# Seven products of halves in place of eight in the feed-forward up and gate products

## The chip, the core and the metric

One core of a Trainium2 chip. The metric is the device time of one execution in microseconds (us); several executions are measured and the median is given. TensorE (PE) multiplies, PEld is its weight load, VectorE is DVE, ScalarE is ACT, GpSimd is POOL, SyncE (SP) issues the transfers.

## The reference, cut to what matters

Two transformer blocks over 512 tokens of width 1024, all in float32. Each has mixers (attention of several kinds, a recurrence) and feed-forward parts, of which there are three:

```python
# first block, hidden width 4096
h2 = rmsnorm(x, norm_ffn_g[l])
x = x + jnp.square(jax.nn.relu(h2 @ w_ff1[l])) @ w_ff2[l]

# second block, twice, hidden width 2816
h = rms_norm(x, ffn_norm[i])
g, u = h @ w_gate[i], h @ w_up[i]
x = x + (jax.nn.silu(g) * u) @ w_down[i]
```

## The kernel before

Everything is kept as [features on 128 partitions, 512 tokens]. Each factor of a dense product is split in two float32r numbers, high = cast(value) on ScalarE and low = value - high on VectorE, and a product is three matmuls: high x high, low weight x high token, high weight x low token (L1075, L1078, L1081), all accumulated in one PSUM bank. Both PSUM and the matmuls work on 128 x 128 weights and 512 token columns.

The work is a list of `Unit`s. A `rows` unit is 128 output features (or 2 or 4 times 128) over `nk` blocks of 128 input features. `Plan.dense` cuts units into ticks: a tick is two weight blocks, that is six matmuls of 512 columns, followed by the steps of the other engines that go with it (`split`, `ev`, ...), some put off by some ticks with `defer`. All five engine programs walk through the same list `plan.steps` in the same order, and each engine does its own part of a step; they are held together by semaphores. So the order on each engine is fixed by hand, and an engine that waits holds up all that it has behind the wait.

Weights come in chunks of 512 KB over SP's queue into `raw0`/`raw1` (L2577); ScalarE casts a chunk to `wh` (L1503, `split`), VectorE makes `wl` (L1856, `split_low`), two buffers of each. The split of chunk n+2 is in the tick in which unit n ends.

A feed-forward stage is `chain(ff)`: groups of four 128-wide hidden tiles (two in the first group of the gated ones). In group c come the up units (in the gated stages gate and up alternate), then the output units of group c-1, which multiply the hidden tiles with the down weights and add to `x` (L2078). The tokens in `hh`, `hl` are not yet divided by their root mean square: the factor, in `W8`, is multiplied in when a bank is evicted (L2026 for relu, L1979 for gate and up). At the start of a stage that factor is not ready, so the first evictions are held back (`hold`). A gate's sigmoid is three dependent ScalarE instructions, Exp, Ln, Exp (L1602, L1612, L1616). Results are split again into the pair `R` (L1588, L1856). `F0` to `F8` are buffers of the mixers, unused within the feed-forward stages. The last output tile of the kernel is done in two halves of 256 tokens (`mm_half`, L1121 to L1123).

The part of the work that GpSimd has is small: additions in the gated mixing and in the recurrence (L2391, L2399, L2415).

Of the kernel before, what the change touches and what calls it, by code (L numbers as in the profile page):

```python
# [7 lines left out]
ALU = mybir.AluOpType  # L8
# [7 lines left out]
P = 128  # L16
T = 512
# [174 lines left out]

class Attn:
# [85 lines left out]
class Plan:  # L279
# [90 lines left out]
    def dense(self, units, more=None, crossed=False, hold=0):  # L370
# [5 lines left out]
        for u in units:  # L376
            if u.kind == "rows":
# [127 lines left out]

    def gate_up(self, n, y):
# [13 lines left out]
    def make(self):  # L520
# [14 lines left out]
        tile, self.f_tile = 0, []  # L535
        for c in range(8):
            self.f_tile.append(tile)
            up = [rows(("w_ff1", 0), 0, 8, c * 512 + j * P, P, ("h", 2), "relu2", f=c, j=j, tile=tile + j) for j in range(4)]
            ff1.append((up, self.out(("w_ff2", 0), 4 * c, 4, ("f", c), norm=2 if c == 7 else None)))
            tile += 4  # L540
        for idx, ff, e, norm in ((0, ff2a, 4, 4), (1, ff2b, 6, None)):
            for c in range(6):
                up, k0, nj, f = [], max(4 * c - 2, 0), 4 if c else 2, 8 + 6 * idx + c
                self.f_tile.append(tile)
                for j in range(nj):
# [3 lines left out]
                                      tile=tile + j)]  # L549
                ff.append((up, self.out(("w_down_2", idx), k0, nj, ("f", f), norm=norm if c == 5 else None,  # L550
# [36 lines left out]
        for units in stages:  # L587
            self.number(units)
# [38 lines left out]
        self.run(self.dense(chain(ff1), roots(1), hold=9))  # L627
# [13 lines left out]
        self.run(self.dense(chain(ff2a), roots(3), hold=9))  # L641
# [18 lines left out]
        self.run(self.dense(chain(ff2b), roots(5, tick=8), hold=10))  # L660
# [89 lines left out]
    dn_tb dn_q dn_s dn_r dn_o dn_p dt_t dt_a""".split()  # L750
# [14 lines left out]
class Memory:  # L765
    def __init__(self, nc, ctx):
# [11 lines left out]
        self.F = {f"F{i}": sb(f"F{i}", 2048) for i in range(9)}  # L778
# [89 lines left out]
    def pair(self, src):  # L868
# [5 lines left out]
        return self.R[2 * n], self.R[2 * n + 1]  # L874

# [165 lines left out]
def tensor_program(pe, S, B, plan):  # L1041
# [67 lines left out]
    def mm_half(u, a, b):  # L1109
# [14 lines left out]
        last.then_inc(S["mm"], 1)  # L1124

# [333 lines left out]
    def dt(u, h):  # L1459
# [10 lines left out]
            "sb": sb, "dt": dt}  # L1470
# [8 lines left out]
def scalar_program(act, S, B, plan, load_table, gains):  # L1479
# [352 lines left out]
    def dt(u, h):  # L1832
# [8 lines left out]
            "c_qt": c_qt, "c_kv": c_kv, "c_kt": c_kt, "sb": sb, "dn_sq": dn_sq, "dn_root": dn_root, "dt": dt}  # L1841
# [8 lines left out]
def vector_program(dve, S, B, plan):  # L1850
# [201 lines left out]
    def tile_low(u, w):  # L2052
# [4 lines left out]
        low(lo[:, js], w[:], hi[:, js], "f_lo")  # L2057

# [637 lines left out]
```

## Time and profile before

| | |
|---|---|
| median of 3 executions | 2140.13 us (2139.98 to 2140.21) |
| profiled execution, first to last instruction | 2138.5 us |
| TensorE busy | 2125.4 us, 99% |
| TensorE weight loads | 1685.6 us, 79% |
| VectorE busy | 1230.8 us, 58% |
| ScalarE busy | 914.8 us, 43% |
| GpSimd busy | 136.4 us, 6% |
| chain that ended last | TensorE 96%, VectorE 2%, ScalarE 1% |

The chain is followed back from the last instruction, at each step to what released it. Records of one engine overlap where it is pipelined: a busy time is that of the union of the records, and a mean is that of a single record.

### The profile page before, as it was taken

Reading aid. Unit: us, or ns where it says so; the run is one execution under the profiler, and the core shown is the slowest. Engines: PE = TensorE matmul, PEld = TensorE weight load, DVE = VectorE, ACT = ScalarE, POOL = GpSimd, SP = SyncE. Lnnn points to the kernel's source line nnn. Section 1 sums busy time; section 2 is a strip of 40 time slices with the busy share of each in tenths; the row PEclk is TensorE's granted clock in tenths of the full one; section 3 lists DMA queues with packets and bytes.
Section 4 is the critical chain, followed back from the end, with each engine's and each line's share of the span. In section 5 each row is a group of like instructions: output and inputs, shape, how many; then the busy total and the mean of one; then the engine's idle time right before and its main releaser. Section 6 shows DMA issues by size and latency. Waiting matters only on the chain.

```text
span 2138.5 us, 27352 instructions
## 1 busy us (share of the span) xinstructions
PE 2125.4 (99%) x10944; PEld 1685.6 (79%) x10944; DVE 1230.8 (58%) x1808; ACT 914.8 (43%) x1449; POOL 136.4 (6%) x174
## 2 busy tenths in 40 slices
PE   9999999999999999999999999999999999999999
PEld 7768778778888888887777888888877668888887
DVE  5584874565544444565676555555556676555554
ACT  4464544554433322334455433333445655333332
POOL 0000432211000000010111000000011100000000
DMA  5213212123222223222112322322221112222223
GB/s 171 84 56 89 61 45 102 40 85 114 98 99 90 98 99 98 99 89 79 60 60 70 99 93 95 99 99 99 89 89 60 59 40 99 99 99 99 89 99 108
DMA packets 52253, 186.91 MB, mean 87 GB/s; under 512 B 5920, under 2 KB 6432, under 8 KB 52000
## 3 DMA queue, kind: packets, MB, share of 16 engines
q1 hardware_dynamic: 51984, 184.99, 26.3%
q8 instruction: 87, 1.43, 0.3%
q14 instruction: 38, 0.31, 0.1%
q10 hardware_dynamic: 144, 0.18, 0.0%
HBM read 183.05 MB, written 2.10 MB: 87 GB/s over the span
## 4 chain that ended last, share of the span: by engine, by line
PE 96%; DVE 2%; ACT 1%; issue 1%; DMA 0%; SPq 0%; DVEq 0%; ACTq 0%
PE ps L1075 24%; PE ps L1078 24%; PE ps L1081 24%; PE ps L1099 4%; PE ps L1102 4%; PE ps L1100 4%; PE ps L1054 3%; PE ps L1171 1%; PE ps L1223 1%; PE ps L1444 1%; PE ps L1426 1%; PE ps L1195 1%; PE ps L1241 1%; PE ps L1316 1%; PE ps L1374 0%
## 5 line engine op out<-in xcount | busy, mean ns | idle before, releaser
L1503 ACT CAST wh<-raw 128x1024 fp32r<-128x1024 f32 x334 | 351.0, 1051 | 866.3 <-PE ps L1081 789.8
L1856 DVE TENSOR_TENSOR wl<-raw,wh 128x1024 fp32r<-128x1024 f32 (+2 forms) x338 | 414.4, 1226 | 187.8 <-ACT wh L1503 187.2
L1075 PE MATMUL ps<-hh,wh 128*128 128x512 f32 x1408 | 447.9, 399 | 1.3 <-DVE F L1994 0.7
L1078 PE MATMUL ps<-hh,wl 128*128 128x512 f32 x1408 | 434.9, 390 | 0.3 <-DVE wl L1856 0.2
L1081 PE MATMUL ps<-hl,wh 128*128 128x512 f32 x1408 | 434.2, 390 | 0.0
L1075 PEld LDWEIGHTS ps<-hh,wh 128*128 128x128 f32 x1408 | 257.5, 188 | 65.9 <-issue 15.1
L1078 PEld LDWEIGHTS ps<-hh,wl 128*128 128x128 f32 x1408 | 264.1, 188 | 57.1 <-DVE wl L1856 1.2
L1081 PEld LDWEIGHTS ps<-hl,wh 128*128 128x128 f32 x1408 | 264.3, 188 | 56.5 <-DVE hl L1937 0.3
L1075 PE MATMUL ps<-R,wh 128*128 128x512 f32 x892 | 285.0, 400 | 0.0
L1078 PE MATMUL ps<-R,wl 128*128 128x512 f32 x892 | 276.1, 390 | 0.5 <-DVE wl L1856 0.5
L1081 PE MATMUL ps<-R,wh 128*128 128x512 f32 x892 | 275.7, 390 | 0.0
L2078 DVE TENSOR_TENSOR x<-ps,x 128x512 f32<-128x512 f32 x191 | 131.0, 689 | 148.3 <-PE ps L1081 148.1
L1078 PEld LDWEIGHTS ps<-R,wl 128*128 128x128 f32 x892 | 167.3, 188 | 36.5 <-DVE wl L1856 1.2
L1075 PEld LDWEIGHTS ps<-R,wh 128*128 128x128 f32 x892 | 163.5, 188 | 41.2 <-issue 9.7
L1081 PEld LDWEIGHTS ps<-R,wh 128*128 128x128 f32 x892 | 167.4, 188 | 35.5
L1099 PE MATMUL ps<-wh,hh 128*128 128x512 f32 (+1 forms) x384 | 155.0, 404 | 0.7 <-DVE F L2005 0.5
L1102 PE MATMUL ps<-wh,hl 128*128 128x512 f32 (+1 forms) x384 | 148.8, 387 | 0.0
L1100 PE MATMUL ps<-wl,hh 128*128 128x512 f32 (+1 forms) x384 | 148.6, 387 | 0.0
L1979 DVE TENSOR_TENSOR ps<-ps,W 128x512 f32<-128x512 f32 x96 | 67.0, 698 | 140.4 <-PE ps L1081 139.2
L1856 DVE TENSOR_TENSOR R<-W,R 128x512 fp32r<-128x512 f32 x84 | 58.1, 692 | 81.8 <-ACT R L1588 78.5
L1099 PEld LDWEIGHTS ps<-wh,hh 128*128 128x128 f32 x384 | 72.1, 188 | 23.0 <-issue 9.5
L1102 PEld LDWEIGHTS ps<-wh,hl 128*128 128x128 f32 x384 | 72.1, 188 | 14.5
(233 smaller groups left out, 1963.7 us busy)
## 6 DMA issues: line engine op xcount, KB each, us to landing
raw<-in_weights SPq DMA_DIRECT2D x332, 512.0 KB, 3.2
x<-in_x_t SPq DMA_DIRECT2D x4, 512.0 KB, 7.2
F<-in_x_t SPq DMA_DIRECT2D x4, 512.0 KB, 4.3
out<-x SPq DMA_DIRECT2D x7, 256.0 KB, 2.0
raw<-in_weights SPq DMA_DIRECT2D x4, 416.0 KB, 3.1
x<-in_bias SPq DMA_DIRECT2D x1, 1024.0 KB, 7.4
F<-in_weights SPq DMA_DIRECT2D x2, 384.0 KB, 3.6
F<-in_weights SPq DMA_DIRECT2D x2, 256.0 KB, 3.9
```

What stands on the lines that cost most here:

```text
L1054: last = pe.transpose(bank[0:rows, i * P:(i + 1) * P], a, ident)
L1075: pe.matmul(out, hi[:, k, cs], B.tile(u.src, k)[0], start=k == 0, stop=False)
L1078: pe.matmul(out, lo[:, k, cs], B.tile(u.src, k)[0], start=False, stop=False)
L1081: last = pe.matmul(out, hi[:, k, cs], B.tile(u.src, k)[1], start=False, stop=k == u.nk - 1)
L1099: pe.matmul(out, B.hh[:, ts], hi[:, kk, :], start=k == 0, stop=False)
L1100: pe.matmul(out, B.hh[:, ts], lo[:, kk, :], start=False, stop=False)
L1102: last = pe.matmul(out, B.hl[:, ts], hi[:, kk, :], start=False, stop=k == 7)
L1171: pe.matmul(bank[:, 0:nk], q[:, qs], k[:, 0:nk], start=True, stop=True).then_inc(S["at_s"], 1)
L1503: act.copy(B.wh[s][:, 0:nk * ncol], B.raw[s][:, 0:nk * ncol]).then_inc(S["w_hi"], 1)
L1856: dve.tensor_tensor(lo, src, hi.bitcast(F32), ALU.subtract).then_inc(S[name], 1)
L1979: dve.tensor_tensor(to[:], B.bank[u.banks[j]][:], B.W[8][:], ALU.mult).then_inc(S["ev_s"], 1)
L2078: dve.tensor_tensor(B.xt(m), bank[:], before, ALU.add).then_inc(S["ev_d"], 1)
```

## The change

From the third pair of 128-wide hidden tiles on (in the first stage from group 2, in the gated stages from the second half of group 1), two neighbouring units become one `Seven`. It multiplies weights of 1024 x 256 with tokens of 1024 x 512, each cut into 2 x 2 blocks (512 input features by 128 outputs, 512 input features by 256 tokens), by Strassen's scheme in Winograd's form: seven products of blocks in place of eight, of which some are of sums of blocks. One product is 12 matmuls with 128 x 128 weights and 256 columns. There are 12 sevens in the first stage and 18 in each of the gated ones.

- Four sums of weight blocks per seven are made on GpSimd (`weight_sums`), from weights that come in one load of 1 MB into `Q0` or `Q1`; each operand of 128 x 512 is then split on ScalarE and VectorE (`weight_high`, `weight_low`) into four rotating buffers, two or three products ahead.
- The sums of token blocks are made once per stage, from tokens that are normalised first (`normed`, `token_sums`, `token_high`, `token_low`, `part_high`, `part_low`), in the ticks that `preparation` names.
- Results are put together from PSUM: ScalarE copies two pieces (`seven_copy`), VectorE adds four (`combine`). Products 2, 4 and 6 wait for such a copy or sum, since they go to a bank, or add to one, that has to be read first.
- `seven_value`, `seven_sigmoid`, `seven_high` and `seven_low` stand for the old evictions.
- Output units are spread: after each seven of the first stage, and after each gate and up of the others, two output units. They rotate over PSUM banks 0 to 2; sevens use banks 3 to 7.
- The buffers of the sums lie in the memory of `F0` to `F8`.

```diff
+PRODUCTS = (("A12", "B21"), ("A11", "B11"), ("A22", "T4"), ("S1", "T1"), ("S2", "T2"), ("S4", "B22"), ("S3", "T3"))
...
+    def seven(self, u, k):
+
+        first, i = [], u.product(k)
+        if k in (2, 5, 6):
+            first.append(("wc", u, {2: 1, 5: 2, 6: 3}[k]))
+        if k in (1, 4):
+            first.append(("wcp", u, {1: 1, 4: 2}[k]))
+        if i + 3 < 7 * (u.last + 1):
+            first.append(("wo_hi", i + 3))
+        if i + 2 < 7 * (u.last + 1):
+            first.append(("wo_lo", i + 2))
+        if k == 5 and u.v + 2 <= u.last:
+            first += [("wq", self.wins[u.v + 2]), ("ws", self.wins[u.v + 2])]
+        if k == 6:
+            self.defer(1, "wc", u, 4)
+            if u.ev == "gate":
+                self.defer(1, "wsig", u, 0)
+                self.defer(2, "wsig", u, 1)
+                self.defer(3, "wf", u, 0)
+                self.defer(4, "wf", u, 1)
+            else:
+                for t in range(2):
+                    self.defer(1 + t, "wf", u, t)
+                    self.defer(1 + t, "wf_hi", u, t)
+                    self.defer(2 + t, "wf_lo", u, t)
+        return first
+
+    def preparation(self, v, stage, wins, tick):
...
+        put(tick + 3, "wq", wins[0])
+        for m in range(8):
+            put(tick + 4 + m, "hn", v, stage, m)
+        for k in range(4):
+            put(tick + 12, "t_sum", stage, k)
+            put(tick + 15 + 2 * k, "t_hi", stage, k)
+            put(tick + 22 + k, "t_lo", stage, k)
+        put(tick + 12, "ws", wins[0])
+        for i in range(3):
+            put(33 + i, "b_hi", stage, i, last_up)
+            put(34 + i, "b_lo", stage, i)
+        put(37, "wq", wins[1])
+        put(37, "ws", wins[1])
+        put(31, "wo_hi", 7 * w)
+        put(32, "wo_lo", 7 * w)
+        put(32, "wo_hi", 7 * w + 1)
+        put(33, "wo_lo", 7 * w + 1)
+        put(36, "wo_hi", 7 * w + 2)
...
@@ def chain(ff):
-            for c in range(1, len(ff)):
-                out += ff[c][0] + ff[c - 1][1]
+            out += [u for u in ff[1][0] if u.kind == "rows"] + ff[0][1] + [u for u in ff[1][0] if u.kind == "win"]
+            for c in range(2, len(ff)):
+                n = len(ff[c][0]) // 2
+                out += ff[c][0][:n] + ff[c - 1][1][:2] + ff[c][0][n:] + ff[c - 1][1][2:]
...
@@ tensor_program
+    def seven(u, k):
+
+        i, (p, q), half = u.product(k), u.banks(), u.v % 2
+        if k == 0:
+            empty(q)
+        elif k == 1:
+            empty(p)
+        elif k == 2:
+            at.wait_ge("w_cp", 2 * u.v + 1)
+        elif k == 4:
+            at.wait_ge("w_c", 4 * u.v + 1)
+        elif k == 5:
+            empty(3)
+        elif k == 6:
+            at.wait_ge("w_c", 4 * u.v + 2)
...
+        for n in range(4):
+            pe.matmul(out, hi[:, n, :], high[:, n, :], start=n == 0 and k not in (4, 6), stop=False, skip_group_check=True)
+        at.wait_ge("b_lo" if name in TOKEN_ORDER else "t_lo", ready)
+        for n in range(4):
+            pe.matmul(out, hi[:, n, :], low[:, n, :], start=False, stop=False, skip_group_check=True)
+        at.wait_ge("wo_lo", i + 1)
+        for n in range(4):
+            last = pe.matmul(out, lo[:, n, :], high[:, n, :], start=False, stop=n == 3, skip_group_check=True)
+        last.then_inc(S["w_mm"], 1)
...
@@ scalar_program
+    def weight_high(i):
+        u, name = plan.wins[i // 7], PRODUCTS[i % 7][0]
+        if i >= 4:
+            at.wait_ge("w_mm", i - 3)
...
+        act.copy(B.operand(i)[0], B.weight_part(u.v, name).rearrange("p (k c) -> p k c", k=4)).then_inc(S["wo_hi"], 1)
...
@@ vector_program
+    def weight_low(i):
...
+        at.wait_ge("wo_hi", i + 1)
+        low(lo, B.weight_part(u.v, name).rearrange("p (k c) -> p k c", k=4), hi, "wo_lo")
...
+    def combine(u, n):
...
+        if n == 1:
+            at.wait_ge("w_cp", 2 * v + 1)
+            at.wait_ge("w_mm", 7 * v + 2)
+            dve.tensor_tensor(a[:, 0:256], p[:, 0:256], a[:, 0:256], ALU.add).then_inc(S["w_c"], 1)
+        elif n == 2:
+            at.wait_ge("w_cp", 2 * v + 2)
+            at.wait_ge("w_mm", 7 * v + 5)
+            dve.tensor_tensor(a[:, 256:512], p[:, 0:256], b[:, 256:512], ALU.add).then_inc(S["w_c"], 1)
...
@@ gpsimd_program
+    def weight_sums(u):
+        at.wait_ge(f"wq{u.v % 2}", 16 * (u.v // 2 + 1))
+        for out, a, b, op in (("S1", "A21", "A22", ALU.add), ("S2", "S1", "A11", ALU.subtract),
+                              ("S4", "A12", "S2", ALU.subtract), ("S3", "A11", "A21", ALU.subtract)):
+            alone()
+            pool.tensor_tensor(B.weight_part(u.v, out), B.weight_part(u.v, a), B.weight_part(u.v, b), op).then_inc(S["w_s"], 1)
+            ran("w_s")
...
@@ sync_program
+    def seven(u):
+        if u.v - u.others[0].v >= 2:
+            at.wait_ge("wo_lo", 7 * (u.v - 1))
...
+        sp.dma_start(B.Q[u.v % 2][:, 0:2048], dram["seven"][size * u.v:size * (u.v + 1)].rearrange("(p n) -> p n", p=P)).then_inc(
+            S[f"wq{u.v % 2}"], 16)
```

## Rows read from the trace of the kernel before

**Rows 1.** The page: busy time, share and instructions; then the chain that ended last

```profile
PE 2125.4 (99%) x10944; PEld 1685.6 (79%) x10944; DVE 1230.8 (58%) x1808; ACT 914.8 (43%) x1449; POOL 136.4 (6%) x174
...
PE 96%; DVE 2%; ACT 1%; issue 1%; DMA 0%; SPq 0%; DVEq 0%; ACTq 0%
```

**Rows 2.** Stretches, the three feed-forward stages: engines' busy us, clock, DMA share, GB/s

```profile
570.00:918.00 348.00, 348.00 (x1535) 287.78 (x1534) 172.89 (x206) 117.97 (x153) 6.81 (x5) 1.00 0.29 97
1166.00:1507.00 341.00, 341.00 (x1505) 281.98 (x1504) 184.34 (x223) 122.31 (x154) 0.00 (x0) 1.00 0.30 98
1785.00:2136.00 351.00, 350.81 (x1556) 290.10 (x1554) 185.37 (x226) 122.18 (x153) 0.00 (x0) 1.00 0.30 98
```

**Rows 3.** TensorE's waits: line, released by, us in all, times, longest

```profile
PE ps L1316 <- DVE F L2227: 3.7, 3, 1.5
...
PE ps L1078 <- DVE wl L1856: 0.8, 2, 0.5
...
PE ps L1054 <- ACT F L1836: 0.2, 1, 0.2
```

**Rows 4.** Timeline of TensorE: start us, us, line, shape, count

```profile
799.62 0.62 PE L1075 MATMUL ps<-R,wh 128*128 128x512 f32 x2
...
800.98 0.62 PE L1075 MATMUL ps<-R,wh 128*128 128x512 f32 x2
...
2132.96 0.28 PE L1122 MATMUL ps<-R,wl 128*128 128x256 f32 x1
...
2133.68 0.28 PE L1122 MATMUL ps<-R,wl 128*128 128x256 f32 x1
```

**Rows 5.** Timeline of TensorE, transposes of 128 columns

```profile
1129.78 0.93 PE L1054 MATMUL ps<-C,F 128*128 128x128 f32 x7
```

**Rows 6.** Timelines of ScalarE and VectorE, then a group by line and form

```profile
1163.80 1.06 ACT L1503 CAST wh<-raw 128x1024 fp32r<-128x1024 f32 x1 [0.58 <-PE ps L1081]
1164.75 0.72 ACT L1522 ACTIVATE hh<-x,G 128x512 fp32r<-128x512 f32 x1
...
1177.75 0.60 ACT L1602 ACTIVATE W<-ps 128x512 f32<-128x512 f32 x1 [0.77 <-DVE ps L1979]
...
1179.14 0.63 ACT L1616 ACTIVATE W<-W 128x512 f32<-128x512 f32 x1
...
1183.26 0.69 DVE L1979 TENSOR_TENSOR ps<-ps,W 128x512 f32<-128x512 f32 x1
1183.86 1.22 DVE L1856 TENSOR_TENSOR wl<-raw,wh 128x1024 fp32r<-128x1024 f32 x1
...
L1659 ACT COPY F<-ps 128x256 f32<-128x256 f32 x16 | 5.9, 371 | 5.1 <-PE ps L1054 4.6
```

**Rows 7.** Timeline where GpSimd and VectorE meet, at three places

```profile
460.97 1.29 POOL L2391 TENSOR_TENSOR x<-x,W 128x512 f32<-128x512 f32 x1 [5.19 <-DVE W L2065]
461.21 2.12 DVE L1856 TENSOR_TENSOR wl<-raw,wh 128x1024 fp32r<-128x1024 f32 x1 [0.32 <-ACT wh L1503]
...
477.78 1.22 DVE L1856 TENSOR_TENSOR wl<-raw,wh 128x1024 fp32r<-128x1024 f32 x1
477.94 2.20 POOL L2391 TENSOR_TENSOR x<-x,W 128x512 f32<-128x512 f32 x1 [2.06 <-DVE W L2065]
...
904.71 1.30 POOL L2399 TENSOR_TENSOR F<-F 128x512 f32<-128x512 f32 x1 [377.14 <-ACT F L1527]
904.72 0.69 DVE L2078 TENSOR_TENSOR x<-ps,x 128x512 f32<-128x512 f32 x1
```

**Rows 8.** Timeline, TensorE starting again after a wait for ScalarE

```profile
1747.55 0.48 ACT L1693 COPY F<-ps 128x384 f32<-128x384 f32 x1 [0.86 <-PE ps L1054]
...
1748.08 0.30 PEld L1259 LDWEIGHTS ps<-W,C 128*128 128x128 f32 x2 [0.80 <-ACT F L1693]
```

**Rows 9.** The page: DMA issues, KB each, median us to landing

```profile
raw<-in_weights SPq DMA_DIRECT2D x332, 512.0 KB, 3.2
...
x<-in_bias SPq DMA_DIRECT2D x1, 1024.0 KB, 7.4
```

More of the change, by code:

```diff
@@ L626, in make, with gated @@
         self.run(self.dense(uO))
-        self.run(self.dense(chain(ff1), roots(1), hold=9))
+        def gated(v, stage, tick=7):
+            more = roots(v, tick=tick)
+            for n, steps in self.preparation(v, stage, [u for u in self.wins if u.stage == stage], tick).items():
+                more.setdefault(n, []).extend(steps)
+            return more
+        self.run(self.dense(chain(ff1), gated(1, 0), hold=9))
         self.run(self.dense(uq[0] + uk[0], roots(2, True, 8), hold=13))
@@ L640, in make @@
         self.run(self.dense(uoS[1]))
-        self.run(self.dense(chain(ff2a), roots(3), hold=9))
+        self.run(self.dense(chain(ff2a), gated(3, 1), hold=9))
         self.add("dn_tables")
@@ new lines, in seven_copy @@
+    def seven_copy(u, n):
+        q = B.bank[u.banks()[1]]
+        a, b = (B.W[i] for i in u.tiles(2 if u.ev == "up" else 0))
+        if n == 1:
+            if u.ev == "up" and u.group:
+                at.wait_ge("w_f", 2 * (u.v - 2) + 2)
+            else:
+                tiles, back = [x.arg["tile"] for x in u.others if "tile" in x.arg], u.group - (4 if u.ev == "relu2" else 2)
+                free = tiles[back] + 2 if back >= 0 else tiles[0]
+                at.wait_ge("f_hi", free)
+                at.wait_ge("f_lo", free)
+            at.wait_ge("w_mm", 7 * u.v + 1)
+            act.copy(a[:, 0:256], q[:, 0:256]).then_inc(S["w_cp"], 1)
+        else:
+            at.wait_ge("w_mm", 7 * u.v + 4)
+            act.copy(b[:], q).then_inc(S["w_cp"], 1)
@@ L1618, in bf, with seven_high @@
+    def seven_high(u, t):
+        j = u.arg["j"] + t
+        at.wait_ge("w_f", 2 * u.v + t + 1)
+        act.copy(B.pair(("f", u.arg["f"]))[0][:, j * T:(j + 1) * T],
+                 B.W[u.tiles(2 if u.ev == "up" else 0)[t]][:]).then_inc(S["f_hi"], 1)
     def bf(u, i):
@@ L2059, in ev_up, with seven_low @@
+    def seven_low(u, t):
+        (hi, lo), j = B.pair(("f", u.arg["f"])), u.arg["j"] + t
+        js = slice(j * T, (j + 1) * T)
+        at.wait_ge("f_hi", u.arg["tile"] + t + 1)
+        low(lo[:, js], B.W[u.tiles(2 if u.ev == "up" else 0)[t]][:], hi[:, js], "f_lo")
     def ev_up(u, j, bank):
```

206 lines of the change are left out of this document (193 added, 13 removed).

## The prediction

> **What bounds the kernel now.** I read the page first. Its busy times say that TensorE works in 99% of the span and that nothing else is above 58% [rows 1]; the chain that ended last is TensorE for 96% [rows 1]. The table of stretches then shows that the three feed-forward stages take 348, 341 and 351 us, TensorE is busy in all but 0.2 us of them, at the full granted clock, and VectorE in about half, ScalarE in a third, GpSimd in almost nothing [rows 2]. The list of TensorE's waits has 13 lines, 10 us together; the longest, 3.7, is the recurrence's, and the first of a dense product has 0.8 [rows 3]. So here time is TensorE's stream, and what shortens that stream shortens the kernel, one for one, until another engine can no longer keep ahead. The reader is to see both: that a cut in matmuls counts in full, and that the slack which hid the other engines' work is what the change spends.
>
> **Cost of a matmul.** In a feed-forward stretch the six matmuls of 512 columns of a tick go from 799.62 to 800.98, 1.36 us, 226.7 ns each [rows 4]. The records of one are 390 ns long because they overlap; the distance between starts is the price. The kernel has one place with 256 columns and fresh weights for each, as in the new code: from 2132.96 to 2133.68 seven matmuls start 0.12 us apart [rows 4]. So 256 columns are not half of 512: some 13 ns of each matmul don't shrink. Columns of 128 with a load each run (0.93-0.27)/6 = 0.11 us apart [rows 5], so a load alone needs about 0.11 us and is still hidden under 0.12, but barely.
>
> **The products.** A pair of 128-column units is 2 x 8 x 3 = 48 matmuls of 512: 48 x 0.2267 = 10.88 us. Seven products of 4 x 3 matmuls of 256 are 84 x 0.12 = 10.08 us. The change takes 12.5% of the columns and 7.4% of the time. There are 12 such sevens in the first stage and 18 (nine gate, nine up) in each of the others, 48 in all: 48 x 0.80 = **38.4 us less**, if TensorE never waits. That is the upper bound of the gain. The Trainium skill ("TensorE: Matmul & The Clock Gate", Back-to-back issue gap) gives a gap of N/2.4 + 2.5 ns, which would be 109 and 216 ns and a saving of about 57 us; the trace's 120 and 227 ns do not agree with it, and I go by the trace.
>
> **What the other engines get.** Independent instructions start closer than their records are long: VectorE 0.60 us for 512 columns (1183.26 to 1183.86), ScalarE 0.95 for 1024 [rows 6], so about 0.55 for 512. For one seven of 10.08 us: ScalarE casts seven weight blocks (7 x 0.55) and copies 256 and 512 columns out of PSUM (0.3 + 0.55), 4.7 us; a gate adds two chains Exp, Ln, Exp of 2.0 us each (1177.75 to 1179.77 [rows 6]), 8.7; relu2 or up adds two casts, 5.8. VectorE: seven low parts 4.2, three sums of 256 and one of 512 1.6, two values 1.2, and two low parts 1.2 unless it is a gate: 7.0 to 8.2. GpSimd: four sums of 1.29 [rows 7], 5.2. All fit on average, and between sevens lie output units of 10.9 us with half of that load. The old evictions and 512-column scalings go away and pay for part. What counts is the order.
>
> *First wait.* Product 2 writes the half bank that product 0 left, and waits for ScalarE's copy. In an up unit, ScalarE's queue is: a cast (0.2 to 0.8 us after the unit's start), the whole first sigmoid chain of the gate before (to 2.77), then that copy (starts 2.67, 0.37 long [rows 6], ends 3.04), then 0.16 until TensorE runs again (ScalarE's record ends at 1748.03, load at 1748.08 and 0.11 of load [rows 8]). Product 2 was due at 2 x 1.44 = 2.88 and starts at 3.20: 0.32 us in each of 18 pairs, **5.8 us**. After output units (first stage, every gate) the copy is over at about 2.1, no wait.
>
> *Second wait.* VectorE and GpSimd get in each other's way. A low part of 1024 columns, normally 1.22 us, took 2.12 when a GpSimd sum had begun 0.24 before it; a like sum, normally 1.29 or 1.30, took 2.20 when the low part was first [rows 7]. Each waits for the other's end. VectorE sums that read PSUM don't suffer (0.69 us beside such a sum [rows 7]). This is what the Trainium skill says ("SBUF — State Buffer", SBUF: two separate sides): an exclusive lock on a shared port pair; the trace agrees in both directions. GpSimd's four weight sums come as a burst when their weights land: the load is issued when the low part of the unit's last block is done, 5.9 us into a unit, 512 KB land in 3.2 us [rows 9]; 97 GB/s at a share of 0.29 [rows 2] are 334 at full, so 512 KB more take 1.6 us more, 4.8. The burst then begins at 10.7, which is 0.6 us into the following unit. For relu2 and for up that is among output units, harmless. For a gate it is in its up unit. There four locks of about 1.15 us push VectorE: low parts of blocks 3, 4, value 0, low part 5, value 1, low part 6 and then the second sum, which product 6 waits for, end near 9.25 in place of before 8; product 6, due at 8.96, starts at 9.4. I take 0.45 us, **8.1 us** in 18 pairs. Bounds: 0 (the burst over before VectorE is needed at 3.6) and 1.9 (it begins 1 to 2 us later, so all 4.6 us of it fall on a VectorE with 2.7 to spare), 0 to 34 us.
>
> *Entries.* Each stage first makes normalised tokens (eight instructions on VectorE, while it also catches up with held evictions), four token sums of 1024 on GpSimd (about 2.6 each by twice 1.29), and their high and low parts. From tick 29 of a stage to tick 40, 11 x 1.36 = 15 us, VectorE has seven low parts of 1024 (8.0), two of weight chunks (2.3), three of 512 (1.8), ten PSUM evictions (6.0), and GpSimd's first burst (4.6, some 2 of it beside evictions): 20.7. It gets 5.7 behind, and three output banks and the two-deep operand queue forgive about 3. Then in the second and third stage two gate-up pairs follow each other with no outputs between, and two more bursts fall on them: another 3. So 6 us twice. The first stage has sixteen ticks of outputs ahead of its first seven: 1.5. Together **13.5 us**; bounds 2 (all hidden) and 25 (each burst in full).
>
> SyncE's queue: a seven's load waits for the low parts of the unit before, and the chunk loads of the next outputs stand behind it; the first of these is due 8 us later, so nothing. Outputs rotate over three PSUM banks in place of four, which leaves two output tiles' time (5.4 us) for an eviction of 0.7.
>
> **Sum.** -38.4 + 5.8 + 8.1 + 13.5 = -11.0. The profiled execution's span is 2138.5 us and the median of the runs 2140.1, 1.6 more; 2127.5 + 1.6 = **2129 us**. The rest of the kernel is untouched: matmuls, queues and DMA bytes (1 MB per seven for two chunks of 512 KB).
>
> **Rivals.** (a) *The slack holds.* The bursts miss and the entries hide: -38.4 + 5.8 + 3 = -29.6, 2110.5. For it: VectorE is busy 52% of the stages [rows 2]; against it: the order above. (b) *GpSimd's lock decides, slower than before.* At 1.9 per pair, 34 + 5.8, entries 18: +19.6, 2159.7. It decides once a pair loses more than (38.4 - 13.5)/18 = 1.4 us where I have 0.8; a load landing 1 us later does it. For it: the 2.12 us record, and the one load of 1024 KB, which took 7.4 us with others before it [rows 9]; against: VectorE's idle start in the up unit. (c) *The sevens do not save.* If a 256-column matmul takes over 10.88/84 = 129.5 ns in the long run, nothing is won; each ns costs 4 us. Against it: the steady 0.12, with the loads at 0.11. Its chance, 0.04, is inside (b)'s. (d) *Gains and waits cancel*, within 0.2% (4.3 us, about what this kernel's runs can tell). (e) *The small matmuls run at the load's pace*, 0.11 us as in [rows 5]: 84 x 0.11 = 9.24, 1.64 x 48 = 79 less, with the waits above -51, 2089. Against it: [rows 4] show 0.12. The formula of the TensorE page of the Trainium skill would put them there.
>
> **Chances.** Forecast (2114 to 2136, without (a)) 0.40; (a) 0.22; (e) 0.02; (d) 0.14; slower, (b) and (c), 0.22. So faster 0.64, same 0.14, slower 0.22. The range for 8 in 10 runs from (a), 2109, into (b), 2148; the likeliest case's own is 2114 to 2136.
>
> **What will show it.** 256-column matmuls 0.12 us apart, 84 per unit. TensorE waiting for ScalarE's 256-column copy some 18 times, 0.3 us each; for VectorE's sums (product 6) or weight low parts in up units, under 1 us each; none in the first stage's sevens. VectorE low parts of 512 in two groups, 0.69 and up to 1.9 us, the long ones in up units. GpSimd busy some 250 us (192 sums of 1.3 to 2) more. Waits of several us at ticks 29 to 45 of the second and third stage. I am wrong if the load lands elsewhere (burst in the outputs: gain near 30), if the lock is dearer, or if the product boundaries cost TensorE time by themselves: 0.12 us at each of 336 would take all.

## The result, and the profile after

The changed kernel takes 2181.83 us (median; 2179.49 to 2183.14), the kernel before beside it 2140.15 us. The ratio is 1.0194 with a 95% interval from 1.0181 to 1.0206: 42 us slower, where 11 us faster was forecast, and outside the range.

The page of the changed kernel answers to [rows 1, 9]:

```profile
PE 2112.5 (97%) x12672; PEld 1743.6 (80%) x12672; DVE 1514.7 (69%) x2213; ACT 1052.5 (48%) x1782; POOL 478.1 (22%) x378
...
PE 80%; DVE 10%; ACT 5%; issue 3%; DMA 1%; SPq 0%; DVEq 0%; ACTq 0%
...
Q<-in_sevens SPq DMA_DIRECT2D x48, 1024.0 KB, 4.9
```

TensorE is busy 12.9 us less and the span is 41.8 us longer: TensorE stands still for 67.8 us of it, 13.1 before. The chain that ended last was 96% TensorE; 20% of it now lies elsewhere, half of that on VectorE. The load of 1 MB takes 4.9 us, where I had worked out 4.8. GpSimd is busy for 342 us more, where I had written some 250.

Where it stands still is seen in the table of stretches (columns as in [rows 2]). First the changed kernel: the entry of the first stage in two parts, its sevens, the entry of the second, and the steady part of the second:

```profile
570.00:605.00 35.00, 33.36 (x143) 26.27 (x141) 24.63 (x32) 15.40 (x21) 4.13 (x2) 1.00 0.30 106
605.00:650.00 45.00, 33.87 (x130) 25.51 (x131) 31.69 (x28) 16.37 (x21) 19.81 (x11) 0.93 0.28 94
650.00:918.00 268.00, 268.00 (x1657) 242.47 (x1656) 198.32 (x262) 106.52 (x168) 65.28 (x42) 1.00 0.26 93
...
1200.00:1262.00 62.00, 48.34 (x261) 40.68 (x260) 53.20 (x57) 30.49 (x45) 28.92 (x15) 0.94 0.22 77
1310.00:1520.00 210.00, 208.36 (x1442) 193.83 (x1441) 162.78 (x225) 110.71 (x186) 80.63 (x56) 1.00 0.26 96
```

The kernel before, in one of these stretches:

```profile
1200.00:1262.00 62.00, 62.00 (x276) 51.32 (x275) 34.73 (x43) 23.33 (x30) 0.00 (x0) 1.00 0.30 101
```

In the sevens of the first stage (from 650) TensorE is never idle, and from 1310 on it is idle for 1.6 of 210 us. From 605 to 650 it is idle for 11.1 us and from 1200 to 1262 for 13.7. There VectorE is busy for 53.2 us of 62, against 34.7 before, GpSimd for 28.9, and the granted clock, 1.00 everywhere before, falls to 0.93 and 0.94.

TensorE's waits (line, released by, us in all, times, longest) answer to [rows 3]:

```profile
PE ps L1236 <- DVE wl L2109: 18.2, 14, 2.9
PE ps L1233 <- DVE x L2394: 10.1, 5, 6.0
PE ps L1307 <- DVE W L2345: 10.0, 18, 1.9
PE ps L1307 <- ACT W L1859: 5.8, 2, 2.9
PE ps L1233 <- ACT wh L1697: 4.4, 1, 4.4
```

L1236 and L1233 are the old kind of product (low weight and high weight), L1307 the first matmuls of a seven's product; `x L2394` is the eviction of an output, `W L2345` the second sum of a seven, `W L1859` ScalarE's copy of 256 columns. Line three has product 6's wait: 12 of its 18 are in steady pairs (0.39 us on the mean), the other six in the first two pairs of each gated stage. The list counts only idle time between two records of more than 0.15 us, so product 2's 0.2 us in every up unit isn't in it; both waits of line four, 2.9 us each, are at the first sevens of the gated stages. The rest belongs to entries too. The wait for `wl` was 0.8 us before and is 18.2 us now.

**The steady pair is as worked out.** The timeline of one up unit, on TensorE, ScalarE, VectorE and GpSimd:

```profile
1317.94 0.64 PE L1313 MATMUL ps<-hh,wx 128*128 128x256 f32 x4
1318.62 0.74 PE L1307 MATMUL ps<-sums_high,wx 128*128 128x256 f32 x4
...
1324.83 0.75 PE L1307 MATMUL ps<-sums_high,wx 128*128 128x256 f32 x4 [0.20 <-DVE W L2345]
...
1318.22 0.35 ACT L1859 COPY W<-ps 128x256 f32<-128x256 f32 x1
...
1321.59 1.65 DVE L2109 TENSOR_TENSOR wx<-Q,wx 128x512 fp32r<-128x512 f32 x1
...
1324.36 0.41 DVE L2345 TENSOR_TENSOR W<-ps,W 128x256 f32<-128x256 f32 x1
...
1316.28 6.41 POOL L2735 TENSOR_TENSOR Q<-Q 128x512 f32<-128x512 f32 x4 [13.76 <-DMA Q<-in_sevens]
```

Four matmuls take 0.48 us, so 0.12 each. From 1317.94 to 1318.62 are 0.68: 0.20 are lost behind ScalarE's copy, which ends at 1318.57 after a sigmoid chain. At 1324.83 product 6 starts 0.36 late behind the second sum, on a VectorE that GpSimd's burst has pushed (1.65 us for a low part of 0.68). This returns every 31.8 us; only the last pair of a stage has no wait for the sum, since no further load of 1 MB, and so no burst, falls on it.

**Sizes of the stages.** I measure a stage from the first addition of squares of its norm (the line in VectorE's `n_add`) to the same of the next part, or, in the last stage, to the end of the last eviction. Before: 349.3, 359.9, 355.5 us. After: 358.1, 375.9, 371.3, together 40.6 more, which is all of the difference. The distances between matmuls beyond 226.7 and 120 ns add up to 19.4, 29.8 and 29.1 us in the three, 78.3; and 78.3 - 38.4 = 39.9. So the matmuls bring what was worked out, and 78 us are lost, of which product 2's waits are 18 x 0.21 = 3.8 and product 6's in the 12 steady pairs 4.7, together 8.5. Some 70 us are lost at three entries, up to and with the first two pairs of a gated stage: 19, 26 and 25 us, where 1.5, 6 and 6 were forecast.

**What an entry looks like.** The second stage's, in the changed kernel. TensorE's timeline around its three longest waits:

```profile
1204.14 0.74 PE L1236 MATMUL ps<-hh,wl 128*128 128x512 f32 x2 [1.78 <-DVE wl L2109]
...
1218.29 0.73 PE L1236 MATMUL ps<-hh,wl 128*128 128x512 f32 x2 [2.87 <-DVE wl L2109]
...
1233.60 1.22 PE L1233 MATMUL ps<-R,wh 128*128 128x512 f32 x2 [5.96 <-DVE x L2394]
...
1248.57 0.74 PE L1307 MATMUL ps<-sums_high,hh 128*128 128x256 f32 x4 [2.89 <-ACT W L1859]
```

GpSimd's timeline in the same stretch, the four token sums and the first burst of weight sums, without a break:

```profile
1206.16 2.40 POOL L2727 TENSOR_TENSOR sums<-Q 128x1024 f32<-128x1024 f32 x1 [62.36 <-DVE Q L2321]
1208.64 3.27 POOL L2727 TENSOR_TENSOR sums<-Q,sums 128x1024 f32<-128x1024 f32 x1
...
1214.46 2.69 POOL L2727 TENSOR_TENSOR sums<-Q,sums 128x1024 f32<-128x1024 f32 x1
1217.30 8.91 POOL L2735 TENSOR_TENSOR Q<-Q 128x512 f32<-128x512 f32 x4
```

VectorE beside it:

```profile
1206.60 3.05 DVE L2109 TENSOR_TENSOR wl<-raw,wh 128x1024 fp32r<-128x1024 f32 x1
...
1212.34 2.60 DVE L2109 TENSOR_TENSOR R<-W,R 128x512 fp32r<-128x512 f32 x1 [0.69 <-ACT R L1782]
1214.86 3.38 DVE L2109 TENSOR_TENSOR wl<-raw,wh 128x1024 fp32r<-128x1024 f32 x1
...
1221.61 5.68 DVE L2109 TENSOR_TENSOR sums_low<-sums,sums_high 128x1024 fp32r<-128x1024 f32 x3
...
1232.86 0.68 DVE L2394 TENSOR_TENSOR x<-ps,x 128x512 f32<-128x512 f32 x1
```

Undisturbed, a low part of 1024 takes 1.22 us and one of 512 0.69. Here they take 3.05, 2.60, 3.38 and, for three, 5.68 where 3.5 is normal: VectorE loses 8 us in these four rows. It is then at its own speed, but so late that the eviction of 1232.86 keeps TensorE waiting for 6 us.

The wait at 1248.57 has another cause, seen in SyncE's and ScalarE's timelines:

```profile
1240.56 0.33 SPq L2962 DMA_DIRECT2D Q<-in_sevens  x1
1240.93 0.43 SPq L2913 DMA_DIRECT2D raw<-in_weights  x1
```

```profile
1246.69 1.04 ACT L1697 CAST wh<-raw 128x1024 fp32r<-128x1024 f32 x1 [7.60 <-DMA raw<-in_weights]
...
1248.16 0.36 ACT L1859 COPY W<-ps 128x256 f32<-128x256 f32 x1
```

The second seven's load stands in SyncE's list ahead of a chunk and waits for the low parts of the tokens, at 1240.48. The chunk leaves behind it and then shares the transfer with 1 MB. ScalarE stands still for 7.6 us in front of its split, and the copy that product 2 needs is queued behind the split.

### The profile page after: what moved, and what is told of

Read it like the earlier page. It is cut to its first block, busy times and chain, and to the rows that moved or that the text cites. A ratio compares the mean times of both kernels' runs of the same rounds, so it can differ in the third digit from the quotient of the medians.

```text
span 2180.3 us, 32023 instructions
## 1 busy us (share of the span) xinstructions
PE 2112.5 (97%) x12672; PEld 1743.6 (80%) x12672; DVE 1514.7 (69%) x2213; ACT 1052.5 (48%) x1782; POOL 478.1 (22%) x378
## 3 DMA queue, kind: packets, MB, share of 16 engines
q8 instruction: 101, 1.65, 0.3%
## 4 chain that ended last, share of the span: by engine, by line
PE 80%; DVE 10%; ACT 5%; issue 3%; DMA 1%; SPq 0%; DVEq 0%; ACTq 0%
PE ps L1233 14%; PE ps L1236 14%; PE ps L1239 13%; PE ps L1307 5%; PE ps L1313 5%; PE ps L1310 5%; PE ps L1257 4%; PE ps L1260 4%; PE ps L1258 4%; PE ps L1212 3%; DVE wl L2109 2%; DMA raw<-in_weights 1%; PE ps L1365 1%; PE ps L1417 1%; DVE hl L2109 1%
## 5 line engine op out<-in xcount | busy, mean ns | idle before, releaser
L1697 ACT CAST wh<-raw 128x1024 fp32r<-128x1024 f32 (+1 forms) x238 | 249.3, 1047 | 471.5 <-PE ps L1239 362.2
L2735 POOL TENSOR_TENSOR Q<-Q 128x512 f32<-128x512 f32 x192 | 309.3, 1611 | 493.7 <-DMA Q<-in_sevens 481.7
L1233 PE MATMUL ps<-R,wh 128*128 128x512 f32 x892 | 289.3, 405 | 16.3 <-DVE x L2394 10.1
L1236 PE MATMUL ps<-R,wl 128*128 128x512 f32 x892 | 278.9, 393 | 4.4 <-DVE wl L2109 4.4
L1233 PE MATMUL ps<-hh,wh 128*128 128x512 f32 x640 | 211.7, 412 | 3.0 <-ACT wh L1703 0.9
L1236 PE MATMUL ps<-hh,wl 128*128 128x512 f32 x640 | 199.6, 393 | 13.8 <-DVE wl L2109 13.7
L1233 PEld LDWEIGHTS ps<-R,wh 128*128 128x128 f32 x892 | 162.5, 190 | 59.5 <-DVE x L2394 12.6
L1236 PEld LDWEIGHTS ps<-R,wl 128*128 128x128 f32 x892 | 168.6, 189 | 42.7 <-DVE wl L2109 6.7
L1239 PE MATMUL ps<-hl,wh 128*128 128x512 f32 x640 | 197.9, 390 | 0.0
L2394 DVE TENSOR_TENSOR x<-ps,x 128x512 f32<-128x512 f32 x191 | 130.4, 685 | 85.1 <-PE ps L1239 85.1
L1236 PEld LDWEIGHTS ps<-hh,wl 128*128 128x128 f32 x640 | 119.2, 188 | 43.9 <-DVE wl L2109 18.7
L2109 DVE TENSOR_TENSOR hl<-Q,hh 128x512 fp32r<-128x512 f32 (+1 forms) x177 | 141.8, 811 | 6.7 <-ACT hh L1822 6.2
L1233 PEld LDWEIGHTS ps<-hh,wh 128*128 128x128 f32 x640 | 113.3, 188 | 38.1 <-issue 16.3
L1239 PEld LDWEIGHTS ps<-hl,wh 128*128 128x128 f32 x640 | 120.1, 188 | 26.6 <-DVE hl L2190 0.2
L2109 DVE TENSOR_TENSOR wx<-Q,wx 128x512 fp32r<-128x512 f32 x168 | 132.7, 800 | 6.7 <-ACT wx L1822 6.3
```

Of the source, the lines that this page charges most:

```text
L1233: pe.matmul(out, hi[:, k, cs], B.tile(u.src, k)[0], start=k == 0, stop=False)
L1236: pe.matmul(out, lo[:, k, cs], B.tile(u.src, k)[0], start=False, stop=False)
L1239: last = pe.matmul(out, hi[:, k, cs], B.tile(u.src, k)[1], start=False, stop=k == u.nk - 1)
L1697: act.copy(B.wh[s][:, 0:nk * ncol], B.raw[s][:, 0:nk * ncol]).then_inc(S["w_hi"], 1)
L2109: dve.tensor_tensor(lo, src, hi.bitcast(F32), ALU.subtract).then_inc(S[name], 1)
L2394: dve.tensor_tensor(B.xt(m), bank[:], before, ALU.add).then_inc(S["ev_d"], 1)
```

## The experiments

Eleven kernels, all with before's runs beside them. "Half clock" is the time between the first and the last instruction in which the trace grants TensorE 0.5.

| kernel | median us | ratio (95%) | stages us | half clock us |
|---|---|---|---|---|
| changed kernel | 2181.83 | 1.0194 (1.0181 to 1.0206) | 358.1, 375.9, 371.3 | 23.9 |
| x1_no_weight_sums | 2157.51 | 1.0085 (1.0070 to 1.0100) | 354.7, 364.6, 360.4 | 21.0 |
| x2_no_gpsimd | 2146.56 | 1.0030 (1.0019 to 1.0041) | 349.7, 361.6, 357.8 | 17.4 |
| x3_load_behind_chunk | 2168.75 | 1.0132 (1.0117 to 1.0147) | 350.0, 374.6, 368.1 | 27.3 |
| x4_neither | 2130.54 | 0.9955 (0.9940 to 0.9970) | 343.8, 357.3, 353.0 | 10.2 |
| x5_sigmoid_later | 2156.77 | 1.0078 (1.0064 to 1.0092) | 349.9, 367.3, 363.0 | 20.5 |
| x6_late_start | 2147.24 | 1.0036 (1.0023 to 1.0048) | 350.8, 363.7, 358.2 | 13.7 |
| x7_both_moves | 2136.83 | 0.9984 (0.9975 to 0.9993) | 349.4, 357.1, 353.2 | 3.4 |
| x8_no_token_lows | 2119.24 | 0.9901 (0.9888 to 0.9915) | 342.2, 353.6, 347.3 | 3.4 |
| x9_refined | 2139.15 | 0.9995 (0.9986 to 1.0004) | 347.9, 358.9, 354.5 | 10.8 |
| x10_load_later_still | 2136.88 | 0.9985 (0.9976 to 0.9994) | 349.8, 356.7, 352.7 | 3.6 |
| x11_load_behind_split | 2133.62 | 0.9968 (0.9956 to 0.9981) | 350.3, 356.2, 351.9 | 6.8 |

**x1_no_weight_sums.** The changed kernel without GpSimd's sums of weights; a block of the weights is split in place of each sum.

```diff
 def weight_sums(u):
-        at.wait_ge(f"wq{u.v % 2}", 16 * (u.v // 2 + 1))
-        for out, a, b, op in (("S1", "A21", "A22", ALU.add), ("S2", "S1", "A11", ALU.subtract),
-                              ("S4", "A12", "S2", ALU.subtract), ("S3", "A11", "A21", ALU.subtract)):
...
+        pass
```

> Leaves out the weight sums: ScalarE and VectorE split plain blocks of the weights where the sums stood, so GpSimd has only the token sums of each stage. The changed kernel took 2181.8 us. Theory L (GpSimd's sums lock VectorE out of a shared port): the 0.35 us wait of product 6 in the gate-up pairs is gone (16 pairs, 6 us), the first burst of each stage (8.9 us long at 1217) no longer delays low parts and evictions, 4 us in each of three stages, and with shorter waits less half-clock time: 2158 to 2166. Theory D (VectorE's own load at the stage entries): only the 6 us go, 2174 to 2178. Theory Q (ScalarE waits for a weight chunk whose load stands behind the 1 MB load on SyncE's queue): the waits of 3.1 to 4.5 us at the first sevens stay.

24.3 us less than the changed kernel, half a microsecond below what theory L gives and far from theory D. The line `DVE W L2345` is gone from TensorE's waits; of the others these remain:

```profile
PE ps L1237 <- DVE wl L2110: 12.9, 11, 2.9
PE ps L1234 <- DVE x L2395: 8.1, 6, 3.8
PE ps L1308 <- ACT W L1860: 5.9, 2, 3.0
PE ps L1234 <- ACT wh L1698: 4.5, 1, 4.5
```

So the weight sums cause the wait of product 6, in the steady pairs (4.7 us) and in the first ones, and a part of the late low parts and evictions; more than half of the 70 us is not theirs. The two waits behind ScalarE are the same as before, so GpSimd is not their cause.

**x2_no_gpsimd.** x1 without the token sums too: blocks of the tokens stand in for them.

```diff
 def token_sums(stage, k):
...
-        a, b = {0: (hn[:, 0:4, second], hn[:, 0:4, first]), 1: (hn[:, 4:8, second], B.token_sum(B.sums, 0)),
...
-        pool.tensor_tensor(out, a, b, ALU.subtract).then_inc(S["t_s"], 1)
+        pass
```

> Leaves out the token sums as well as the weight sums: plain blocks of the tokens are split in their place, so GpSimd does nothing in the feed-forward stages, and ScalarE, VectorE and TensorE do as much as before. Theory L: VectorE's low parts are all back at 0.69 and 1.22 us, and the waits for weight low parts at ticks 19 to 30 of each stage (2.8, 3.0 and 3.0 us) go too: 2145 to 2155. Theory D: 2165 or more, since VectorE still has eight normalisations and seven low parts of 1024 at each entry. Theory Q: 9 to 12 us of waits behind the 1 MB load remain, plus half-clock time behind them.

Another 11.0 us less, for 12 instructions of GpSimd. All that GpSimd does in this change is thus worth 35.3 us, and without it the kernel is still 6 us slower than before.

**x3_load_behind_chunk.** Only the order on SyncE: the second seven's 1 MB stands two ticks later, behind the chunk. It computes the whole reference.

```diff
-        put(37, "wq", wins[1])
-        put(37, "ws", wins[1])
+        put(39, "wq", wins[1])
+        put(39, "ws", wins[1])
```

> Computes all. The second seven's load of 1 MB is put two ticks later in the list (39 for 37), behind the weight chunk of that tick on SyncE's queue. Theory Q: ScalarE's wait of 7.6 us for a chunk at 1246.7 and its likes in the other stages go, and with them TensorE's 4.5, 3.1 and 3.1 us and the half-clock stretches near them: 12 to 20 us less than 2181.8, 2162 to 2170. Theory L or D: nothing, 2180 to 2183, since VectorE is late there anyway.

13.1 us less than the changed kernel. ScalarE's split at the same place, which had waited 7.60 us for its chunk, now waits only for TensorE, and the copy follows it:

```profile
1235.14 1.05 ACT L1697 CAST wh<-raw 128x1024 fp32r<-128x1024 f32 x1 [4.25 <-PE ps L1239]
...
1236.65 0.37 ACT L1859 COPY W<-ps 128x256 f32<-128x256 f32 x1
```

In the list of waits the lines `ACT wh L1697` and `ACT W L1859`, 10.2 us, are gone; `DVE W L2345` rises from 10.0 to 14.2, since the weight sums now run later. In the first stage 8.1 us stay won, in the second 1.3 and in the third 3.2. The edit also puts the weight sums later, so this run alone can't tell the two apart; x4 against x2, where there are no such sums, can: 16.0 us.

**x4_neither.** x2 and x3 together.

> As x2 (no sums on GpSimd, plain blocks in their place) and the load moved as in x3. If L and Q together are the cause, the entries cost little: 38.4 less than before for the matmuls, 18 pairs of 0.21 and some 2 us at each entry: 2108 to 2118. If D has a large part: 2130 or more.

51.3 us less than the changed kernel, where 35.3 and 13.1 make 48.4: two causes that add up. The kernel is 9.7 us faster than before, and still loses 30 us of its stages (5.2, 12.3 and 12.5) without GpSimd and with the loads in order. VectorE's low parts of the token sums now take their own time:

```profile
1204.04 3.48 DVE L2114 TENSOR_TENSOR sums_low<-Q,sums_high 128x1024 fp32r<-128x1024 f32 x3
```

**x8_no_token_lows.** x4 without the seven low parts of the tokens (of the four sums and the three blocks); the products take the blocks of `hl` that are there, and the second seven's load waits for the high parts in place of the low ones.

```diff
-            put(tick + 22 + k, "t_lo", stage, k)
+            pass
...
-            put(34 + i, "b_lo", stage, i)
+            pass
```

> x4 (2130.5 us: no sums on GpSimd, load moved) and also without the low parts of the seven token operands (old low parts of other tokens stand in), so VectorE has 8 us less to do between ticks 29 and 37 of each stage; TensorE has as many matmuls. Theory D (what is left in x4 is VectorE's own load at the entries): the waits for its evictions (4.2 and 3.8 us) and low parts (2.3, 1.9, 1.7) and the half-clock time behind them shrink by half or more: 2116 to 2123. If these waits come from earlier (normalisations, held evictions): 2126 to 2130.

Another 11.3 us less, for 21 instructions of VectorE, 24 us of its work. The stretch of the entry in x4 and, below, in x8:

```profile
1190.00:1262.00 72.00, 67.92 (x435) 61.82 (x434) 56.04 (x84) 45.42 (x72) 0.00 (x0) 0.95 0.28 96
```

```profile
1190.00:1262.00 72.00, 70.68 (x464) 64.68 (x463) 50.91 (x81) 46.95 (x74) 0.00 (x0) 0.99 0.33 115
```

TensorE is idle for 4.1 and 1.3 us there. So VectorE's own work at the entry is a third cause, apart from the other two. One thing is not kept apart: with the low parts gone, the second seven's load leaves 4 to 7 us earlier in its stage. But in x4 TensorE's long waits are for VectorE's evictions and none is for a load.

**x5_sigmoid_later.** x3 with the gate's sigmoid chains and values some ticks later, behind the copy of product 2. It computes the whole reference.

```diff
-                self.defer(1, "wsig", u, 0)
-                self.defer(2, "wsig", u, 1)
-                self.defer(3, "wf", u, 0)
-                self.defer(4, "wf", u, 1)
+                self.defer(2, "wsig", u, 0)
+                self.defer(5, "wsig", u, 1)
+                self.defer(4, "wf", u, 0)
+                self.defer(7, "wf", u, 1)
```

> Computes all. x3 (2168.75 us) with the two sigmoid chains of a gate put later in the list: the first behind the up unit's 256-column copy, the second behind its 512-column copy. If the waits of the steady pairs are what I read them as, the 0.21 us of product 2 go (18 pairs, 4 us) and most of the 0.35 of product 6 with them (VectorE then has less queued before its second sum; x3 lost 17 us to that sum in all): 2156 to 2164. If product 6 waits for VectorE's lock alone: 2164 to 2166.

12.0 us less than x3. Behind `ACT W` the stages lose 0.8 us in place of 3.8, and behind `DVE W L2345` 7.9 in place of 17.2, for the values no longer stand in front of the second sum; most of what is left of that is in the first two pairs of a stage. Both waits of the steady pair are a matter of order, and all but a little of them can be had back for nothing.

**x6_late_start.** The changed kernel with the preparation drawn out over more ticks and the first seven at tick 56 of a gated stage in place of 40 (16 sevens in place of 18, which costs 4 x 0.8 = 3.2 us of TensorE); the first weight sums wait for the token low parts. x3's order isn't in it: the second seven's 1 MB, at tick 52 (44 in the first stage), still leaves ahead of the chunk (at 1244.44 and 1244.81). It computes the whole reference.

```diff
-            put(tick + 4 + m, "hn", v, stage, m)
+            put(tick + 4 + 2 * m, "hn", v, stage, m)
-            put(tick + 12, "t_sum", stage, k)
-            put(tick + 15 + 2 * k, "t_hi", stage, k)
-            put(tick + 22 + k, "t_lo", stage, k)
+            put(tick + 19, "t_sum", stage, k)
+            put(tick + 22 + 2 * k, "t_hi", stage, k)
+            put(tick + 29 + (2 * k if stage else k), "t_lo", stage, k)
...
-        put(37, "wq", wins[1])
+            put(52, "wq", wins[1])
...
+            put(44, "wq", wins[1])
...
     def weight_sums(u):
+        if u.v == u.others[0].v:
+            at.wait_ge("t_lo", 4 * u.stage + 4)
```

> Computes all. The changed kernel with more room at the entries: gated stages keep group 1 in single units, so that the first seven comes at tick 56 for 40 (16 sevens for 18 in each, 3.2 us of the gain given up); normalisations every second tick, token sums, their parts and the first weight sums later, the weight sums behind the low parts of the token sums; the second 1 MB load in the last ticks before the first seven. If crowding (L, Q and D together) at the entries is the cause of 60 of the 80 us lost, most of it goes: waits at entries 20 instead of 55, half-clock time under 10 us: 2125 to 2145. If the loss is in the sevens themselves: 2165 or more.

34.6 us less than the changed kernel (7.3, 12.2 and 13.1 in the stages), with the same instructions on GpSimd and VectorE but for the four sevens; that is 2 us above the range expected, and 13.7 us of half clock are left where under 10 were expected. It is 21.5 less than x3, although it lacks x3's edit. So a large part of the loss comes from the same work standing too close together, and not from its amount.

**x7_both_moves.** x6 with x5's order of the sigmoids.

> x6 with the later sigmoid chains of x5: 6 to 9 us less than x6, so 2118 to 2138. Below 2140 it beats both kernels.

2136.83 us over 11 runs: 10.4 less than x6 where 6 to 9 were expected, 45 us less than the changed kernel and 0.16% less than the kernel before, with the interval just below one. Its waits:

```profile
PE ps L1249 <- DVE wl L2122: 5.1, 8, 1.5
PE ps L1320 <- ACT W L1872: 4.7, 3, 3.5
...
PE ps L1246 <- DVE x L2407: 3.5, 5, 0.8
PE ps L1320 <- DVE W L2358: 3.3, 4, 1.2
```

**x9_refined.** x7 with the first stage's preparation drawn out further, its weight sums later still, and the gated stages' low parts of the blocks a little later.

```diff
-            put(tick + 29 + (2 * k if stage else k), "t_lo", stage, k)
+            put(tick + 29 + 2 * k + (0 if stage else 3), "t_lo", stage, k)
...
-                put(end + 2 + i, "b_lo", stage, i)
+                put(end + (2, 3, 5)[i], "b_lo", stage, i)
...
-                put(40 + i, "b_hi", stage, i, last_up)
-                put(41 + i, "b_lo", stage, i)
+                put(34 + 2 * i, "b_hi", stage, i, last_up)
+                put(35 + 2 * i, "b_lo", stage, i)
...
-            put(44, "wq", wins[1])
-            put(44, "ws", wins[1])
+            put(39, "wq", wins[1])
+            put(42, "ws", wins[1])
```

> x7_both_moves with the first stage's preparation drawn out too: there the high and low casts of the tokens that a seven reads stand at ticks 34 to 38, the low parts of the token sums behind them, the second seven's load of 1 MB at tick 39, and the gated stages' low parts two to five ticks later. Theory (work piled up in the entries, each of VectorE and SyncE late by some us): the first stage's waits of 2.0 us for a VectorE low part and 3.65 us behind ScalarE's split go, half of the gated stages' 3.0 and 2.4 us waits for x go too, in all 4 to 8 us less than x7: 2128 to 2134 us, some 0.4% less than before. Rival (what is left is not the order but the amount of VectorE work at an entry): the waits only move by some ticks, 2136 to 2138 us.

The theory was wrong: 2139.15 us, 2.3 more than x7 and 1 more than the rival's range. The waits moved, as the rival said; that the amount of VectorE's work is the reason is not shown by this run. The first stage wins 1.5 us, and the gated ones lose 1.8 and 1.3. There the last low part of the blocks ends later against the start of its stage, the 1 MB waits for it and the chunk stands behind the 1 MB, so product 2 loses 2.6 and 2.5 us in place of 0.8 each. Moved by a tick or two, the waits of an entry only change their name:

```profile
PE ps L1320 <- ACT W L1872: 4.8, 2, 2.4
...
PE ps L1326 <- DVE wx L2122: 3.4, 2, 2.2
```

**x10_load_later_still.** x7 with x3's edit once more: the second seven's load at tick 54 for 52 (46 for 44 in the first stage).

> x7_both_moves with the second seven's 1 MB load and its weight sums two ticks later in every stage (tick 54 for 52, 46 for 44), so that it stands behind the next chunk in SyncE's list. In x7 ScalarE still stands 7.6 us in front of a split at 1241 to 1249 whose chunk was issued behind that 1 MB, and the first stage loses 3.65 us behind it. Theory (SyncE's order is a cause of its own, also once the entries are drawn out): the waits behind ScalarE's copy go from 3.5 us and 0.8 us twice to nearly nothing, 3 to 6 us less than x7: 2131 to 2134 us. Rival (the second seven's weights and sums are then late themselves): the wait moves to product 1 or 6 of the second seven, 2136 to 2139 us.

2136.88 us, x7's time, and the same waits. Neither theory was tried: the chunk is issued at the last tick ahead of the seven, 55 and 47, so the order on SyncE was still the old one (1 MB at 1243.41, chunk at 1243.78), as in x7 (1243.20 and 1243.57). The run is of use as a repetition of x7, 0.05 us away from it.

**x11_load_behind_split.** The same to tick 55 and 47, which does change the order.

```diff
-            put(52, "wq", wins[1])
-            put(52, "ws", wins[1])
+            put(55, "wq", wins[1])
+            put(55, "ws", wins[1])
...
-            put(44, "wq", wins[1])
-            put(44, "ws", wins[1])
+            put(47, "wq", wins[1])
+            put(47, "ws", wins[1])
```

> x7_both_moves with the second seven's 1 MB load at tick 55 for 52 (47 for 44 in the first stage), which puts it behind the next chunk in SyncE's list in every stage; two ticks later, as in x10, had left the list as it was, since the chunk stands at the last tick ahead of the seven. Theory (SyncE's order is a cause of its own, also once the entries are drawn out): ScalarE's 7.6 us in front of the split go, the waits behind its copy go from 3.6, 0.8 and 0.8 us to nearly nothing, 3 to 6 us less than x7: 2131 to 2134 us. Rival (the second seven's weights and sums are then late themselves): the wait moves to the second seven's second sum or to its operands, 2136 to 2139 us.

2133.62 us, 3.2 less than x7 and 6.5 less than the kernel before (0.3%): it beats both and computes the whole reference. ScalarE's split no longer waits for its chunk but for TensorE, 6.0 us in place of 7.6, and the line `ACT W` is gone from TensorE's waits:

```profile
1248.53 1.05 ACT L1710 CAST wh<-raw 128x1024 fp32r<-128x1024 f32 x1 [6.02 <-PE ps L1252]
```

The rival holds in the first stage: 3.6 us behind the copy go, but 1.6 us for `wl`, 1.4 for a second sum and some 1.5 for matmuls at half clock come, and the stage is 0.9 us longer than in x7. The gated stages are 0.9 and 1.3 us shorter.

## Why the prediction was wrong

**The products: right.** 256 columns go at 0.12 us (3625 of 4004 distances are 0.120), not at the N/2.4 + 2.5 ns that the Trainium skill gives for a single matmul ("TensorE: Matmul & The Clock Gate", Back-to-back issue gap); -38.4 us is what the stages show once their waits are taken out. Rivals (c) and (e) are out.

**First wait: right**, with its mechanism and its 18 places; 0.21 us each for 0.32, 3.8 us for 5.8. x5 took it away by moving the sigmoid chain.

**Second wait: right in the steady pairs**, 0.39 us for 0.45, but in 12 of 18 pairs: 4.7 us. The last pair of each stage has none; in the first two pairs of the gated stages it is 0.7 to 2.0 us, 6.4 together, which I count with the entries. All 18 make 11.1 us for 8.1. The sevens of the first stage have none, as forecast. x1 shows that the weight sums cause it, and x5 that it also needs the values ahead of the second sum. Rival (b), 1.9 us in every pair, is out, although its 2159.7 us lies nearer than my number; its mechanism was there in those four pairs. The lock itself (the Trainium skill, "SBUF — State Buffer", SBUF: two separate sides) holds with all the records above: a low part of 512 took up to 1.80 us for 0.68, and GpSimd's 192 sums 1.61 us on the mean for 1.29.

**Entries: the step that failed.** I had 13.5 us, with 25 as the upper bound; it was about 70. The step took each engine's load at an entry as nearly hidden, and three parts of it were wrong.

- *The window was drawn too late and its beginning counted as free.* I set VectorE's load against tick 29 to 40. The first waits, at 1204 and 1218, come at ticks 20 and 28 of the stage, before and beside the token sums, and I had not charged the token sums with any lock, only the first weight burst, "some 2 of it". Four instructions of 2.4 us and more, one behind the other, and then the burst, held GpSimd from 1206 to 1226 and took 8 us from VectorE in four rows. x2 against x1 puts 11 us on these 12 instructions, and x1 puts 24 on the weight sums, 20 of them outside the steady wait.
- *"SyncE's queue: ... so nothing".* I looked at a seven in the steady state, where the load waits for the seven before. At an entry the second load waits for the last token low part, which is late there, and the chunk behind it was needed at once. x3 shows 13 us, by an edit of two numbers, and x4 against x2 16; where the entries are already drawn out, x11 shows 3. What is behind a waiting transfer was named and priced with the wrong due time.
- *The slack of VectorE was a guess.* "Three output banks and the two-deep operand queue forgive about 3" was subtracted from a lateness of 5.7 us. The trace doesn't show such slack: in x4 VectorE works without a break from 1209.6 to 1221.9, and TensorE waits 4.0 us, until 1213.83, for an eviction out of that row of work. x8 against x4 shows that 24 us of VectorE work at three entries cost 11 us, where GpSimd does nothing and TensorE has no long wait for a load.

Of the 70 us, the runs thus account for some 31 by GpSimd (35 less the 5 of the steady pairs), 13 to 16 by SyncE's order (x3 alone, x4 against x2), and 11 by VectorE's low parts. What is left, some 12 to 15 us, is not separated: in x8 the stages still lose 19 us beyond the ideal spacing, 4 of them in product 2's steady wait and 1.5 that the kernel before had too. Another 5 us are four waits for `wl` at ticks 16 to 20, ahead of any token sum, where VectorE makes the normalised tokens beside the held-back evictions; no run takes these away by themselves.

**The forecast as a whole.** A step that works out 0.3 us per pair to the hundredth stood beside a bound of 25 us for the entries that was itself only an estimate of one stage's lateness. The share of slower, 0.22, was all given to a mechanism of the steady state.

## What to carry to other kernels

Where a change needs its operands prepared once per stage, lay out that stretch engine by engine from its first instruction, with the slowed durations where two engines share a port, before costing the steady state: here the waits of the steady pairs were right to 5 us and three entries wrong by 56. On an in-order queue, ask for every waiting transfer what stands behind it at the place where its condition comes latest, not where it comes usually. And a saving of 38 us on the engine that bounds the kernel is worth moving the first use later, even at the price of some repetitions: drawing the preparation out and giving up four sevens (3.2 us) brought 34.6, without a change in SyncE's order.

## What the runs showed of the hardware

**TensorE's granted clock halved after waits.** In the kernel before it is 1.00 in all stretches. In the changed kernel it is 0.5 for 23.9 us in five places, and 512 columns go 0.43 us apart in place of 0.227 there. Two stretches that include such places, and TensorE's timeline in the second:

```profile
643.00:650.00 7.00, 5.42 (x12) 3.83 (x13) 4.66 (x4) 1.43 (x2) 3.73 (x3) 0.52 0.25 75
1292.00:1295.40 3.40, 3.40 (x15) 3.12 (x14) 2.16 (x5) 0.00 (x0) 0.00 (x0) 0.53 0.90 314
```

```profile
1293.97 1.05 PE L1233 MATMUL ps<-R,wh 128*128 128x512 f32 x2
1294.82 0.82 PE L1236 MATMUL ps<-R,wl 128*128 128x512 f32 x2
1295.48 0.63 PE L1239 MATMUL ps<-R,wh 128*128 128x512 f32 x2
```

That is the lower of its two levels (1.2 GHz of 2.4). Ahead of 643.44 TensorE had been idle for 4.4 us, ahead of 1233.60 for 6.0. Ahead of 1292 the longest wait was 1.8 us, and from 1284 to 1292 it was busy for 6.2 of 8 us. The other two places begin at 1875.5, in a wait of 2.9 us, and at 1919.9, after one of 1.9. After the 2.87 us at 1218.29 the clock stayed at 1.00. The matmuls at half clock cost about 7 us of the 78 beyond their waits (21 distances of 512 columns with 0.2 us more each and 28 of 256 columns with 0.09 more, a part of the 23.9 us being idle anyway). It went with the waits: 3.4 us of half clock are left in x7, behind a wait of 3.5 us. No run here took the halving away and kept the waits, so its share is read from the spacing alone.
